# A routed-expert block: no sorting pass, each job's rows gathered in the job in front of it

## The reference, cut to what matters

```
scores = sigmoid(x @ w_router)                      # 256 tokens x 16 experts
sel = scores + router_bias
grp_score = top_k(sel.reshape(4 groups, 4), 2)[0].sum(-1)   # sum of the two best of each group
masked = where(repeat(one_hot(argmax(grp_score))), sel, -1e30)
_, idx = top_k(masked, 2)                           # two experts inside the best group
gates = chosen / sum(chosen)
for e in range(16):
    y += combine[:, e] * ((silu(x @ w_gate[e]) * (x @ w_up[e])) @ w_down[e])   # 2048 -> 1024 -> 2048
return h + mod5 * y
```

## Time and profile before

| what | value |
|---|---|
| time, median of 3 runs | 1483.64 us (1482.21 to 1486.89) |
| profiled execution | 1487.16 us, span 1485.3 us |
| busy in the span | PE 84%, DVE 29%, ACT 10%, POOL 5% |
| moved by DMA | 559.39 MB, mean 377 GB/s |
| chain that ended last | PE 47%, DMA 44%, DVE 5%, issue 2% |
| mean granted PE clock | 0.947 |

### The profile page before, as it was taken

One profiled execution on the slowest core, in us unless ns is written; L12 is line 12 of the kernel. 1 busy time (PEld: TensorE's weight loads), 2 busy tenths in 40 slices (PEclk: granted clock), 3 DMA queues, 4 the chain that ended last, 5 costly groups with the idle time before them and its releaser, 6 DMA issues.

```text
span 1485.3 us, 18646 instructions
## 1 busy us (share of the span) xinstructions
PE 1243.5 (84%) x7756; PEld 530.1 (36%) x7757; DVE 430.4 (29%) x812; ACT 147.7 (10%) x255; POOL 76.2 (5%) x138
## 2 busy tenths in 40 slices
PE   3899999899999999879969969978768767857855
PEld 2555644455445564323323323222222221221221
DVE  3211696577655351111110210111111111111112
ACT  3000100234200032100000000000000000000000
POOL 0111200011222000000000000000000000000000
PEclk9899999999999999999999989999988989988988
DMA  9999668666789778899999999999999999999996
GB/s 374 419 389 390 274 234 336 234 229 242 255 329 387 288 283 359 340 426 428 424 428 429 428 428 429 426 428 427 429 429 428 428 429 428 428 429 428 428 427 289
DMA packets 56849, 559.39 MB, mean 377 GB/s; under 512 B 6624, under 2 KB 6624, under 8 KB 19680
## 3 DMA queue, kind: packets, MB, share of 16 engines
q1 hardware_dynamic: 41904, 502.48, 81.1%
q0 software_dynamic: 14320, 52.01, 9.4%
q10 hardware_dynamic: 576, 4.19, 0.7%
HBM read 556.57 MB, written 2.10 MB: 376 GB/s over the span
## 4 chain that ended last, share of the span: by engine, by line
PE 47%; DMA 44%; DVE 5%; issue 2%; ACT 1%; DVEq 0%; ACTq 0%; POOL 0%; SPq 0%
DMA ring<-w_gate_dram 11%; DMA ring<-w_up_dram 10%; PE ps L860 8%; PE ps L855 7%; PE ps L578 7%; DMA ring<-w_down_dram 5%; DMA big<-w_up_dram 5%; PE ps L887 4%; DMA ring<-w_half_dram 4%; DMA big<-w_gate_dram 4%; PE ps L681 3%; DMA ring<-w_in_dram 3%; PE ps L572 3%; PE ps L881 2%; PE ps L821 2%; PE ps L583 2%
## 5 line engine op out<-in xcount | busy, mean ns | idle before, releaser
L855 PE MATMUL ps<-ring,early 128*32 128x256 f32 x1888 | 125.3, 407 | 50.0 <-DMA ring<-w_up_dram 22.5
L860 PE MATMUL ps<-ring,early 128*64 128x512 f32 x560 | 138.7, 631 | 22.5 <-DMA ring<-w_gate_dram 11.9
L1566 DVE TENSOR_TENSOR big<-ps,big 128x1024 f32<-128x1024 f32 x60 | 70.7, 1219 | 267.8 <-PE ps L802 142.1
L578 PE MATMUL ps<-ring,big 128*128 128x512 f32 x320 | 146.0, 598 | 0.0
L1190 DVE SCALAR_TENSOR_TENSOR once<-ring,silu_c,once 128x1024 f32<-128x1024 f32 x96 | 123.2, 1283 | 45.5 <-DMA ring<-w_half_dram 38.7
L881 PE MATMUL ps<-ring,once 128*32 128x512 f32 x576 | 87.2, 722 | 45.3 <-DMA ring<-w_down_dram 45.1
L681 PE MATMUL ps<-ring,big 128*128 128x512 f32 x256 | 115.6, 609 | 1.3 <-ACT big L1075 1.3
L855 PEld LDWEIGHTS ps<-ring,early 128*32 128x32 f32 x1888 | 57.9, 115 | 130.4 <-issue 47.0
L578 PEld LDWEIGHTS ps<-ring,big 128*128 128x128 f32 x320 | 59.1, 191 | 69.4 <-issue 69.3
L855 PE MATMUL ps<-big,early 128*32 128x256 f32 x800 | 57.6, 431 | 29.8 <-DMA big<-w_up_dram 20.9
L887 PE MATMUL ps<-ring,once 128*64 128x512 f32 x336 | 77.3, 598 | 2.3 <-DMA ring<-w_down_dram 2.3
(11 more groups left out here) (320 smaller groups left out, 1031.4 us busy)
## 6 DMA issues: line engine op xcount, KB each, us to landing
ring<-w_down_dram SPq DMA_DIRECT2D x48, 2048.0 KB, 25.6
ring<-w_up_dram SPq DMA_DIRECT2D x47, 2048.0 KB, 25.3
ring<-w_gate_dram SPq DMA_DIRECT2D x32, 2048.0 KB, 25.5
ring<-w_half_dram POOLq DMA_DIRECT2D x96, 512.0 KB, 6.4
big<-w_up_dram SPq DMA_DIRECT2D x17, 2048.0 KB, 22.7
ring<-w_mix_dram SPq DMA_DIRECT2D x32, 1024.0 KB, 12.1
big<-w_gate_dram SPq DMA_DIRECT2D x16, 2048.0 KB, 25.5
late<-w_down_dram SPq DMA_DIRECT2D x16, 2048.0 KB, 23.7
```

The lines of the kernel that those rows point to most:

```text
L578: mm = pe.matmul(ps[:, b + t, :], nT[:, k, t * P:(t + 1) * P], w, start=(k == 0), stop=(k == KT - 1))
L855: mm = pe.matmul(out_b[0][BASE * f:BASE * (f + 1), :], rows[0][:, k, :], w[:, kk, f * 256:(f + 1) * 256], start=(k == 0), stop=(k == KT - 1))
L860: mm = pe.matmul(out_b[1][REST * f:REST * (f + 1), :], rows[1][:, k, :], w[:, kk, f * N:(f + 1) * N], start=(k == 0), stop=(k == KT - 1))
L1566: tt(y, Yb[:, 2 * h:2 * h + 2, :].rearrange("p a n -> p (a n)"), y, ALU.add).then_inc(summed, 1)
```

## The change

- The sorting pass, its one-hot matrices and the positions among all 512 rows go. `gather_next` picks, in each job, the 96 rows of the next job, 16 blocks of 96 columns, four blocks behind each of the down chunks 1 to 4; ACT saves them with scale and bias in 16 instructions of 96 columns, in place of one copy of 1536.
- The sums go to `total`, a copy of `tokens` that ACT makes in job 0, since `tokens` is now read in every job.
- The memory of the sorted rows becomes a seventh pair buffer in the loop, at one place of the twelve (`next_pairs`). Job 0's pairs get the same buffers in the same order of issue, but other weights in them.
- PE's list: logits blocks 1 and 2 stand in front of the last `wout` chunk; four `busy` products instead of two in front of `route` 1, none behind it.
- DVE: pairs of instructions become one `scalar_tensor_tensor` for each half, the sum of the two best of a group is found without the minima, and the expert ranks go. Positions and counts have a semaphore step each.

```diff
-             (2, 2): [("half", 4)], (3, 1): [("half", 5)], (3, 2): [("shift",), ("logits", 0)],
-             (3, 3): [("logits", 1), ("shift_rows",), ("logits", 2)]}
+             (2, 2): [("half", 4)], (3, 1): [("half", 5)], (3, 2): [("shift",), ("logits", 0), ("logits", 1), ("logits", 2)],
+             (3, 3): [("shift_rows",)]}
...
-        "slots": one * np.arange(2 * SEQ)[None],
+        "slots": one * np.arange(BLK)[None],
...
-        job_pairs += [big[:, SORTED + 2 * CH:SORTED + 4 * CH], big[:, SORTED:SORTED + 2 * CH], once[:]]
-        first_pairs = (6, 8, 0, 1, 2, 3, 7, 4, 5, 0, 1, 2)
+        job_pairs += [nT_all[:, 0:2 * CH], big[:, TT * D:2 * TT * D], once[:]]
+        total = nT_all[:, 0:TT * D].rearrange("p (t d) -> p t d", t=TT)
+        first_pairs = (0, 1, 8, 2, 3, 6, 7, 4, 5, 0, 1, 2)
+        next_pairs = (3, 4, 7, 0, 1, 2, 3, 4, 5, 0, 1, 2)
...
+        def last_use(p):
+
+            s = next_pairs[p]
+            if s in next_pairs[:p]:
+                return 2 * max(q for q in range(p) if next_pairs[q] == s) + 1
+            return 2 * max(q for q in range(JPAIR) if s in (first_pairs[q], next_pairs[q])) + 1 - JCH
...
-            for i, s in enumerate(first_pairs):
+            for i in (5, 2, 0, 1, 3, 4, 6, 7, 8, 9, 10, 11):
...
-                    sp.wait_ge(slot_free, used_job(2 * (i - 7) + 1))
+                    sp.wait_ge(slot_free, used_job(2 * first_pairs.index(s) + 1))
...
-                    sp.wait_ge(slot_free, j * JCH + used_job(2 * i + 1 - JOB_SLOTS))
+                    sp.wait_ge(slot_free, j * JCH + used_job(last_use(i)))
...
-                        pe.wait_ge(shift_ready, 1)
-                        pe.matmul(T[:, 2 * NE:3 * NE], ones, rt[:, 18, 0, :], start=True, stop=True).then_inc(pos_done, 1)
...
-            def sort_rows(blocks):
-                pe.wait_ge(oh_ready, 1)
-                for k in blocks:
-                    if k > 1:
-                        pe.wait_ge(sorted_saved, k - 1)
+            def gather_next(j, i):
+
+                if i == 0:
+                    pe.wait_ge(oh_ready, j + 1)
+                if i % 2 == 0:
+                    pe.wait_ge(summed, j * 4 + (3 + i // 2))
+                for k in range(4 * i, 4 * i + 4):
+                    at = k % 4 * BLK
                     for t in range(TT):
-                        mm = pe.matmul(S[k % 2], tokens[:, t, k * P:(k + 1) * P], oh_all[:, t, :],
+                        mm = pe.matmul(Yb[:, i, at:at + BLK], tokens[:, t, k * P:(k + 1) * P], oh_rows[:, t, :],
                                        start=(t == 0), stop=(t == TT - 1))
-                    mm.then_inc(sort_done, 1)
+                mm.then_inc(next_gathered, 1)
...
                     mm.then_inc(slot_free, 1)
+                    if 1 <= i <= 4:
+                        gather_next(j, i - 1)
...
                 if first:
-                    save_sorted(range(0, KT // 2))
+                    act.wait_ge(slot_free, used_job(2 * first_pairs.index(6) + 1))
+                    for t in range(TT):
+                        last = copy(total[:, t, :], tokens[:, t, :])
+                    last.then_inc(total_ready, 1)
...
-                job_rows(at)
+
+                for k in range(KT):
+                    if k % 4 == 0:
+                        act.wait_ge(next_gathered, j * 4 + (k // 4 + 1))
+                    at = k % 4 * BLK
+                    last = act.activation(xg[:, k, :], Yb[:, k // 4, at:at + BLK], ACT.Identity,
+                                          bias=modcol[:, 3, k, 0:1], scale=scale_ffn[:, k:k + 1])
+                last.then_inc(xg_ready, 1)
...
-                link(tt(eq, values, mx.unsqueeze(2).broadcast_to(shape), ALU.is_equal))
-                link(tt(eq, eq, numbers.unsqueeze(1).broadcast_to(shape), ALU.mult))
+                for t in range(TT):
+                    last = stt(eq[:, t, :], values[:, t, :], mx[:, t:t + 1], numbers, ALU.is_equal, ALU.mult)
+                link(last)
...
-            link(tt(rt[:, 17], rt[:, 19], T[:, 2 * NE:3 * NE].unsqueeze(1).broadcast_to([P, TT, NE]), ALU.add))
-            both = rt[:, 20:22]
-            link(tt(both, rt[:, 12:14], rt[:, 17:18].broadcast_to([P, 2, TT, NE]), ALU.mult))
-            place4 = small[:, 6:10].rearrange("p (i t) -> p i t", i=2)
-            link(nc.vector.tensor_reduce(place4, both, AX.X, ALU.add))
...
                 last.then_inc(hidden_ready, 1)
+                for t in range(TT):
+                    last = ts(oh_rows[:, t, :], k_("slots"), job[:, 0, t, bass.ds(j + 1, 1)], rs_tok[:, t:t + 1],
+                              ALU.is_equal, ALU.mult)
+                last.then_inc(oh_ready, 1)
```

More of the change, by code:

```diff
@@ L102, in make_schedule @@
             seq += after.get((g, c), [])
-    seq += [("busy", 2), ("hT", 3), ("busy", 1), ("logits", 3), ("gate_b", 0), ("gate_b", 1), ("busy", 2),
-            ("route", 1), ("busy", 1)]
+    seq += [("busy", 2), ("hT", 3), ("busy", 1), ("logits", 3), ("gate_b", 0), ("gate_b", 1), ("busy", 4),
+            ("route", 1)]
     for k in range(KT):
@@ L317, in build @@
         landed = [sem(f"landed{i}") for i in range(SLOTS)]
-        job_landed = [sem(f"job_landed{i}") for i in range(PAIR_SLOTS + 3)]
+        job_landed = [sem(f"job_landed{i}") for i in range(len(job_pairs))]
         slot_free = sem("slot_free")
@@ L431, in _ @@
                 sp.wait_ge(out_ready, q + 1)
-                sp.dma_start(out[t * P:(t + 1) * P, a:b], tokens[:, t, a:b]).then_inc(out_sent, 16)
+                sp.dma_start(out[t * P:(t + 1) * P, a:b], total[:, t, a:b]).then_inc(out_sent, 16)
             sp.wait_ge(out_sent, 16 * len(OUT_PIECES))
@@ L723, in _ @@
                         pe.matmul(T[:, NE:2 * NE], ones, mask[:, 0, :], start=True, stop=False)
-                        pe.matmul(T[:, NE:2 * NE], k_("before"), mask[:, 1, :], start=False, stop=True)
+                        pe.matmul(T[:, NE:2 * NE], k_("before"), mask[:, 1, :], start=False, stop=True) \
+                            .then_inc(pos_done, 1)
                         for t in range(TT):
-                            mm = pe.matmul(T[0:CAND, 128:129], cand[:, t, 0, :], ones[:, 0:1],
+                            pe.matmul(Z[1][0:CAND, 128:129], cand[:, t, 0, :], ones[:, 0:1],
+                                      start=(t == 0), stop=(t == TT - 1))
+                        for t in range(TT):
+                            mm = pe.matmul(Z[1][0:1, 130:131], cand[:, t, 0, FIRST_EXPERT:FIRST_EXPERT + 1], ones[:, 0:1],
                                            start=(t == 0), stop=(t == TT - 1))
-                        for t in range(TT):
-                            pe.matmul(T[0:1, 130:131], cand[:, t, 0, FIRST_EXPERT:FIRST_EXPERT + 1], ones[:, 0:1],
-                                      start=(t == 0), stop=(t == TT - 1))
-                        pe.wait_ge(shift_ready, 1)
-                        pe.matmul(T[:, 2 * NE:3 * NE], ones, rt[:, 18, 0, :], start=True, stop=True).then_inc(pos_done, 1)
+                        mm.then_inc(pos_done, 1)
                     elif part == 2:
@@ L862, in experts @@
                         mm.then_inc(slot_free, 1)
-                if first:
-                    sort_rows(range(0, KT // 2))
-                else:
+                if not first:
                     scatter(j, 1, parts=ahead)
@@ L876, in experts @@
                 for i in range(8):
-                    if i == 4 and first:
-                        sort_rows(range(KT // 2, KT))
                     w = arrived(16 + i)
@@ L1100, in _, with job_evac @@
             act.wait_ge(table_ready, 1)
-            jobs = act.value_load(n_i[0:1, 4 * JOBS:4 * JOBS + 1], min_val=2, max_val=JOBS - 1)
-            def job_rows(at):
-                span = big[:, bass.ds(at + SORTED, KT * 2 * SEQ)].rearrange("p (k s) -> p k s", k=KT)
-                return copy(xg, span[:, :, 0:BLK]).then_inc(xg_ready, 1)
-            def save_sorted(blocks):
-                for k in blocks:
-                    act.wait_ge(sort_done, k + 1)
-                    act.activation(xg_all[:, k, :], S[k % 2], ACT.Identity, bias=modcol[:, 3, k, 0:1],
-                                   scale=scale_ffn[:, k:k + 1]).then_inc(sorted_saved, 1)
-            def job_evac(j, parts, at, first):
+            jobs = act.value_load(n_i[0:1, NUMBERS:NUMBERS + 1], min_val=2, max_val=JOBS - 1)
+            def job_evac(j, parts, first):
                 act.wait_ge(slot_free, j * JCH + used_job(7))
@@ L1455, in _ @@
             last.then_inc(mask_ready, 1)
-            for i, n in ((2, 16), (4, 17)):
-                last = tt(rt[:, n], k_("e16").unsqueeze(1).broadcast_to([P, TT, NE]),
-                          small[:, i:i + 2].unsqueeze(2).broadcast_to([P, TT, NE]), ALU.is_gt)
-            link(last)
-            link(tt(rt[:, 16], rt[:, 16], rt[:, 17], ALU.add))
-            tt(rt[:, 18, 0, :], rt[:, 16, 0, :], rt[:, 16, 1, :], ALU.add).then_inc(shift_ready, 1)
```

(1 more changed line is left out.)

149 lines of the change are left out of this document (63 added, 86 removed).

## The result

The changed kernel takes 1494.87 us (median of 20 runs, 1485.65 to 1502.61), the kernel before, on the same chip, 1485.81 us (20 runs, 1478.52 to 1493.05). The ratio is 1.0059, 95% interval 1.0040 to 1.0078: some 9 us slower, where +1.4 was forecast. The time lies just inside the range given ("from above 1495"), and outside the forecast's own 1481 to 1490.

What follows compares the result with a forecast made beforehand. The weight stream (DMA, 427 to 429 GB/s) bounds the second half. Earlier stream start -16.1, smaller table -0.3, stops in full jobs +17.8: +1.4 us on the median 1483.64 gives 1485.0; range from below 1475 to above 1495.

Steps and rivals of the forecast that it cites:

- the terms named for the upper end: Reasons for a range end above 1495: margins at zero in full jobs, +4.5 us, and low-clock logits, +3.6.
- Routing behind the last chunk: Front, first routing step to job 0: ten linked DVE instructions fewer, job 0 starting at 551.0, 2.4 us earlier.
- The signs named for the front: Expected in the profile after: last `wout` chunk near 518.5, first routing step near 534.5, job 0's first product near 551.
- I take neither: Clock around the moved logits: neither 1.8 us regained nor 3.6 us added was counted; routing starts 1.0 us late.
- slower, by the logits: Rival, PE from 513 to 528: clock stays low through moved logits and chunk, 3.6 us more, 1490; chance 0.22.
- The stops: Ends of the three full jobs: pairs 4 and 5 issued 7.44 us later, DMA stops 6.7 + 4.7 + 6.3 = 17.8 us.
- the margins that the prediction read: Ends of the three full jobs in the kernel before: DMA 0.7, 2.7 and 1.1 us from running dry.
- the 0.9 of ramp: Job 0's transfer with bytes from 553.7: DMA's ramp at a restart costs 0.9 us.
- Gathers elsewhere cost nothing: Light and middle jobs: PE waits for DMA there, so 7.44 us of gathers a job cost nothing.
- Hidden gathers: Rival: 14.5 us of idle PE in a light and full job together hides the gathers, 1467; chance 0.13.
- The pace by columns: Rival, gathers in jobs: paced by their columns, 5.2 us a job, stops 11.1 us, 1478.3; chance 0.08.
- The clock in the gathers: Rival, full jobs: gathers lower the clock and double to 14.9, three stops of 7 us more, 1507; chance 0.05.

Runs made afterwards that it cites:

- e1: The changed kernel with logits blocks 1 and 2 back behind the last `wout` chunk: 1490.0 us, ratio 1.0017 to the kernel before.
- e6: The changed kernel with only one gather block of four in the last job, whose gathered rows nobody uses: 1491.42 us, ratio 1.0046.
- e7: The changed kernel with the three full jobs gathering their next rows twice, all others once: 1518.28 us, ratio 1.0244.
- e8: The changed kernel run again, with no edit: 1495.46 us, ratio 1.0092 to the kernel before.
- e10: e4 with the full jobs' gathers moved behind down chunks 4 to 7: 1479.58 us, ratio 0.9958.
- e2: The changed kernel with full jobs gathering one of four blocks behind each of down chunks 1 to 4: 1482.12 us, ratio 0.9961.
- e5: The changed kernel with light and middle jobs except job 0 gathering twice, full jobs once: 1518.01 us, ratio 1.0253.
- e3: The changed kernel with `next_pairs` reordered, so pairs 4 to 6 wait for the chunk pair seven in front, not six: 1475.57 us, ratio 0.9923.
- e4: The changed kernel with the edits of e1 and e3 together: 1474.73 us, ratio 0.9906.

## Why the prediction was right within its range, and 8 us off

The mechanism was as forecast: a start of the stream 13 us earlier, given back in three stops at the ends of the full jobs, for the reason named (all four gathers stand in front of down chunk 5, whose release issues pair 4). The size was not. The sum had +1.4 us and the profiles have +10.3: 3.1 less gained in front, 2.6 more in the stops, 2.9 at the end, and the table's 0.3, which the account doesn't show apart.

That 1494.87 still lies in the range is in part luck: it is 0.1 us inside (on the forecast's own base, 1483.64, the 9.1 us would give 1492.7), and the terms named for the upper end (4.5 and 3.6 on 1485.0) reach 1493.1 only. The end of the kernel, 2.9 us, stood in none of them. "Slower" by more than 0.3% had 0.35, less than the 0.44 for no change. Step by step:

- **Routing behind the last chunk: right to 0.1 us a step.** First routing step to `route` 6.08 us (537.46 to 543.54; forecast 6.1), `route` to first gather 1.73 (forecast 1.7), gather to job 0 8.70 (8.7), to pair 9 2.0 (1.9), from there 36 us to pair 4 of job 1, which the account takes over and the bytes bear out. In e1 pair 9 stands 39.9 behind `shift`; the prediction's 552.9 is 40.7 behind it. (In e6, e7 and e8 `route` came 7.7 us behind the first routing step: there PE's own products were last, the gate rows at the lower clock.) The signs named for the front came 2 to 3 us late: chunk at 520.55 for 518.5, routing at 537.46 for 534.5, job 0 at 553.97 for 551.
- **The logits' clock: the term that was mis-sized.** The step "I take neither" put nothing on the clock. It took 18.4 - 15.1 = 3.3 us, and `route` came that much later. That is the rival "slower, by the logits" in size (3.6) and place. It had 0.22, and e1 shows 4.2 us for the move as a whole where the step had a loss of 1.0. In other executions of the same list the clock took 1.4 (e7) to 3.2 us (e8) up to pair 9, in the chunk or in the gate rows behind it: the term varies from run to run, and with the logits back e10 still lost 1.5 us. So the clock's share is shown for each profile, and that the move alone brings it is not. The rule of the Trainium skill's page "TensorE: Matmul & The Clock Gate" (The HAM clock gate, What's actually happening), idle first and then 1.2 GHz, would have had the chunk in 7.03 to 7.11; the trace disagrees in this place, PE being busy in all of 512 to 526.
- **The stops: 20.4 for 17.8.** The pace was 16 instructions from 694.74 to 696.69, 122 ns each and not 116: 7.8 us a job, three times 0.4. The rest is in the margins. In the kernel before, the three full jobs take from first gate product to first down product 52.06, 50.42 and 52.06 us:

```profile
651.44 1.89 PE L855 MATMUL ps<-ring,early 128*32 128x256 f32 x16 [2.97 <-DMA ring<-w_gate_dram]
...
703.50 1.06 PE L881 MATMUL ps<-late,once 128*32 128x512 f32 x8 [0.95 <-ACT once L1123]
...
768.92 1.07 PE L855 MATMUL ps<-ring,early 128*32 128x256 f32 x16 [1.36 <-DMA ring<-w_gate_dram]
...
819.34 1.06 PE L881 MATMUL ps<-late,once 128*32 128x512 f32 x8 [0.95 <-ACT once L1123]
```

  The 1.65 us between them goes with the wait of 3 us in front (the first product takes 1.89 for 1.07, the lower clock), and it is nearly the difference of the margins that the prediction read (0.7, 2.7, 1.1) without asking why they differ. In the changed kernel's profile no full job starts so, in e8 the first two do (52.06), and its first two stops are 8.0 us each by windows of 6 us, for 6.0 and 7.0. With margins of 2.4 to 2.8 for jobs that start at full clock the stops should be 5.0 to 5.4 and are 6.0 to 7.0. Of each, 0.6 to 1.9 us are left open, and e2 kept 12 us of stops with a quarter of the gathers; the 0.9 of ramp that the prediction charged at the restart and not here would fit, and no run tests it.
- **Gathers elsewhere cost nothing: right, by 0.26 us.** e5 shows how near it was: 1.00 of the wait of 1.26 is DVE's and stays. The prediction gave no number for that cover.
- **The end: +2.9, absent from the sum.** The prediction ended its sum with the stream. In the profiles the wait in front of the last scatter is 1.7 longer (3.10 for 1.38) and the scatter, at the lower clock, 1.2 (3.21 for 2.00). The wait comes with the change, and its cause is open.
- **The rivals.** The logits and their clock are above. Hidden gathers fell: e7 is one to one. The pace by columns fell: 122 ns, and not 82. The clock in the gathers fell: 1.00 through the stop. The seventh buffer could hide most of the stops, but at another place of the table (e3).

Two versions beat both kernels, and can't be told apart: e3, with the seventh buffer at pair 3, and e4, which has the logits as they were besides. The prediction said that from slice 18 on DMA stays at 427 to 429 GB/s; the earlier trace rows has 424 to 429, which changes nothing in it.

## What to carry to other kernels

Where a stream of weights bounds a kernel, the price of added work is not its share of an engine's idle time but what stands in front of the next release of a buffer; read the margin at that one place, for each kind of stage, and at the end of the stage in front. Before work is taken out or hidden, try the order in which the buffers are handed on: here a table of twelve numbers was worth 14 us of stops. And count a chain of short products as a risk to the clock of what follows, with a value of its own in the sum.

## What the runs showed of the hardware

- Behind and in short products with a weight load of 128 columns each TensorE can be at 0.50 (1.2 GHz) with no idle between them, as from 516 to 524 in the changed kernel: 48 of them took 5.68 to 8.55 us in nine profiles of moved logits, where one block of 16 took 1.96, and the chunk of 512 columns behind them took 8.5 to 9.7, at full clock 7.11. In the same program the length differs from one execution to the next (7.97 and 7.34 in two of the changed kernel), and so does the place: in e1 the chunk ran at full clock and the four products behind the logits took 3.20 us for 1.96.
- Idle time does it as well: over all profiles, 23 full jobs entered behind waits of 1.0 to 2.1 us took 50.4 us to the first down product; of 19 behind 2.8 us and more, 16 took 52.0 or longer and three 50.4. In kind this agrees with the rule of the Trainium skill's page "TensorE: Matmul & The Clock Gate" (The HAM clock gate, What's actually happening), idle first and then 1.2 GHz. So idle time in front of a bound stage can cost 1.65 us, and a change that shortens the job before can lose a part of its gain there (e1, e2).
- A gather instruction of 96 columns took 122 ns in the loop, at full clock.
